# Feed-forward of a hybrid decoder layer: order of the second norm's row, a weight rounding and three stored products

## Chip, cores and metric

The kernel runs on one core of one Trainium2 chip, as one program. Its time is the device time of one execution in microseconds (us); the number compared is the median of several runs.

## What is computed

One layer for 512 prompt tokens and 32 sample tokens (8 sequences of 4), model width 1024: a Conformer convolution branch and an mLSTM branch, merged by gates, then the part that the change is in:

```python
x = x + rmsnorm(jnp.einsum('btd,de->bte', mix, w_o), g_post_mix)
hf = rmsnorm(x, g_pre_ff)
ff = jnp.einsum('btf,fd->btd', jnp.square(jax.nn.relu(jnp.einsum('btd,df->btf', hf, w_ff1) + b_ff1)), w_ff2) + b_ff2
x = x + rmsnorm(ff, g_post_ff)
```

`w_ff1` is 1024 x 4096 and `w_ff2` is 4096 x 1024. `rmsnorm` divides by the root of the mean square over the 1024 features. All is float32.

## The kernel before

Activations lie with features on the 128 partitions and all 544 tokens (`TT`) along a row. Every weight matrix is cut into chunks of 1024 x 128 that arrive in one stream of 176 chunks. For float32 precision each chunk is split in two: `hi` on ScalarE (ACT) rounds it from `wraw` to `whi` (L511), `lo` on VectorE (DVE) subtracts to `wlo` (L846). SyncE's queue (SP) loads chunks into two `wraw` buffers and waits for DVE's roundings; `whi` and `wlo` are rings of four. A product of one chunk with the activations (`part`, `product`, L1311) is three terms (hi x hi, hi x lo, lo x hi) for each of 8 feature tiles, each in two pieces of 256 and 288 columns: 24 groups of two matmuls. Products are written in turn to two PSUM slots. `chunk_done` counts finished products, `drained[s]` counts how often slot `s` has been emptied, and TensorE (PE) waits for `drained[s]` before it writes the slot again. On each engine the instructions run in the order of the program; there is no scheduler.

The feed-forward part takes `w_ff1` in two halves (`f`), each with 16 chunks up and 16 chunks down (`HID` is 16). Up products of the first half begin before the norm of their input is known: the operand is `x * g_pre_ff` without the norm's row `rst`, and each product is multiplied by `rst` afterwards. The first three chunks are multiplied side by side, tile by tile as the operand appears, into the two slots and the spare banks of `side`. ACT copies these three to `kept`. The sums of squares (`column_sums`) follow the fourth product on PE, and `root(4, ...)` on ACT makes `rst` out of them (a table load L524, a logarithm L526, an exponential L528).

Before the change ACT copies and rounds in turn, and then takes the root:

```python
for k in range(3):
    act.wait_ge(chunk_done, C_FF + k + 1)
    act.activation(kept[:, k:k + 1, :], slot(k) if k < 2 else spare(), ACT.Copy).then_inc(drained[k % 2], 1)
    hi(0, 4, C_FF + 4 + k)
root(4, stat_ready, 2)
```

For every up product there is then a chain between DVE and ACT: DVE multiplies by `rst` into `fr` (L1266 for the stored ones, L1269 for the fourth, L1280 in the loop), ACT applies bias and ReLU (L791), the square (L793) and a rounding copy to `hidhi` (L795), and DVE subtracts to `hidlo` (L1260). The three stored products go through it first, then the fourth, and then a loop (`Fori`) of three turns of four products follows, which also rounds the weights of the product three ahead. `hid_hi` and `hid_lo` count finished tiles. The down products (`double`) use all 16 tiles, and their first turn waits tile by tile for `hid_lo`.

Of the kernel before, what the change touches and what calls it, by code (L numbers as in the profile page):

```python
# [32 lines left out]
HID = 16  # L33
# [9 lines left out]
C_FF = C_OUT + KT  # L43
# [18 lines left out]
S_FF = S_OUT + KT // 2  # L62
# [51 lines left out]
def hybrid_layer(nc, xT, wstream, w_gates, cols, b_gates, b_v, w_dw, hist, c_in, n_in, m_in,  # L114
                 yT, conv_p, conv_s, c_p, n_p, m_p, c_s, n_s, m_s):
    f32, f32r = mybir.dt.float32, mybir.dt.float32r
    ALU = mybir.AluOpType
# [5 lines left out]
    with ctx:  # L123
# [180 lines left out]
        def c(name, j):  # L304

            return col[:, bass.ds(COLS[name] + j, 1)]

        def tile(buf, j, lo=0, n=TT):

            return buf[:, bass.ds(j, 1), lo:lo + n]  # L310
# [23 lines left out]
        def own_columns(ap):  # L334

            return bass.AP(ap.tensor, ap.offset, [ap.ap[0], [NS + DEC_T, DEC_B], [1, DEC_T]])

        def spare(lo=0, hi=TT):
            return across(side[:, 2:4, :], lo, hi).rearrange("p (a t) -> p a t", a=1)

# [4 lines left out]
        def slot(s, lo=0, hi=TT):  # L345

            return across(psum[s][:, :, :], lo, hi).rearrange("p (a t) -> p a t", a=1)
# [157 lines left out]
        def _(act):  # L505
            def hi(i, per, k):

                act.wait_ge(raw_in[k % 2], 8 * per * i + 16 * (k // 2 + 1))
                if k >= RING:
                    act.wait_ge(chunk_done, per * i + (k - RING + 1))  # L510
                act.activation(whi[:, k % RING, :, :], wraw[:, k % 2, :, :], ACT.Copy).then_inc(hi_done, 1)  # L511
# [6 lines left out]
                    apart(act)  # L518
                act.activation(fr[:, k:k + 1, :], src, ACT.Square).then_inc(sq_ready, 1)

            def root(n, sums, count):


                act.preload_act_table_set("natural_log_exp_and_others")  # L524
                act.wait_ge(sums, count)
                act.activation(rst[:, :], across(side[:, 0:2, :]), ACT.Ln, bias=eps[:, :], scale=1.0 / D_MODEL).then_inc(ms_ready, 1)  # L526
                act.wait_ge(ms_ready, n)
                act.activation(rst[:, :], rst[:, :], ACT.Exp, scale=-0.5).then_inc(root_ready, 1)  # L528
# [254 lines left out]
            for k in range(3):  # L783
                act.wait_ge(chunk_done, C_FF + k + 1)
                act.activation(kept[:, k:k + 1, :], slot(k) if k < 2 else spare(), ACT.Copy).then_inc(drained[k % 2], 1)
                hi(0, 4, C_FF + 4 + k)
            root(4, stat_ready, 2)

            def hidden(n, i, k):

                act.activation(fr[:, k % 2, :], fr[:, k % 2, :], ACT.Relu, bias=c("b_ff1", n)).then_inc(hid_pos, 1)  # L791
                act.wait_ge(hid_pos, n + 1)
                act.activation(fr[:, 2 + k % 2, :], fr[:, k % 2, :], ACT.Square).then_inc(hidsq_ready, 1)  # L793
                act.wait_ge(hidsq_ready, n + 1)
                act.activation(tile(hidhi, 4 * i + k), fr[:, 2 + k % 2:3 + k % 2, :], ACT.Copy).then_inc(hid_hi, 1)  # L795

            for k in range(4):
                if k < 3:
                    act.wait_ge(hid_scaled, k + 1)
                else:  # L800
                    act.wait_ge(drained[1], S_FF + 2)
                hidden(k, 0, k)

            for f in range(2):
                cf = C_FF + PERHALF * f
                sf = S_FF + S_HALF * f
                with act.Fori(1 - f, HID // 4) as i:
                    for k in range(4):
                        hi(i, 4, cf + k + 3)
                        act.wait_ge(drained[k % 2], 2 * i + (sf + k // 2 + 1))  # L810
                        hidden(4 * i + (HID * f + k), i, k)

                def down(i, ks):
                    for k in range(4):
                        if k in ks:
                            hi(i, 4, cf + HID + k + 3)
                        if k % 2 == 1:
                            j = 2 * i + k // 2
                            if f == 0:
                                act.wait_ge(chunk_done, 4 * i + (cf + HID + k + 1))  # L820
                                act.activation(tile(sgm, j), slot(k // 2), ACT.Identity, bias=c("b_ff2", j)).then_inc(drained[k // 2], 1)
                            else:
                                act.wait_ge(drained[k // 2], i + (sf + HID // 2 + 1))
                                squares(4 * KT + j, tile(y, j), k // 2)

                turns = KT // 2 - f
                with act.Fori(0, turns) as i:
                    down(i, range(4))
                if f == 1:
                    down(turns, range(1))  # L830
# [4 lines left out]
        def _(dve):  # L835
# [411 lines left out]
            for j in range(KT):  # L1247
# [2 lines left out]
                V.tensor_tensor(sqs[:, :], sqs[:, :], fr[:, j % 4, :], ALU.add).then_inc(sq_added, 1)  # L1250
                if j == 3:
                    lo(0, 4, C_FF + 3)
            for k in range(3):
                lo(0, 4, C_FF + 4 + k)
            dve.wait_ge(root_ready, 4)

            def remainder(n, i, k):

                dve.wait_ge(hid_hi, n + 1)
                V.tensor_tensor(tile(hidlo, 4 * i + k), fr[:, 2 + k % 2:3 + k % 2, :], tile(hidhi, 4 * i + k).bitcast(f32),  # L1260
                                ALU.subtract).then_inc(hid_lo, 1)

            for k in range(4):
                if k < 3:
                    dve.wait_ge(drained[k % 2], S_FF + k // 2 + 1)
                    V.tensor_tensor(fr[:, k % 2:k % 2 + 1, :], kept[:, k:k + 1, :], rst3, ALU.mult).then_inc(hid_scaled, 1)  # L1266
                else:
                    dve.wait_ge(chunk_done, C_FF + 4)
                    V.tensor_tensor(fr[:, 1:2, :], slot(1), rst3, ALU.mult).then_inc(drained[1], 1)  # L1269
                remainder(k, 0, k)  # L1270
            n = mark(V.memset(sqs[:, :], 0.0))
            dve.wait_ge(dve_step, n)
            for f in range(2):
                cf = C_FF + PERHALF * f
                sf = S_FF + S_HALF * f
                with dve.Fori(1 - f, HID // 4) as i:
                    for k in range(4):
                        lo(i, 4, cf + k + 3)
                        dve.wait_ge(chunk_done, 4 * i + (cf + k + 1))
                        V.tensor_tensor(fr[:, k % 2:k % 2 + 1, :], slot(k % 2), rst3, ALU.mult).then_inc(drained[k % 2], 1)  # L1280
                        remainder(4 * i + (HID * f + k), i, k)

                def down(i, ks):
                    for k in range(4):
                        if k in ks:
                            lo(i, 4, cf + HID + k + 3)
                        if k % 2 == 1 and f == 1:
                            s, j = k // 2, 2 * i + k // 2
                            dve.wait_ge(chunk_done, 4 * i + (cf + HID + k + 1))
                            V.tensor_tensor(tile(y, j), slot(s), tile(sgm, j), ALU.add).then_inc(drained[s], 1)  # L1290
                            dve.wait_ge(sq_ready, j + (4 * KT + 1))
                            dve.wait_ge(sq_added, j + 4 * KT)
                            V.tensor_tensor(sqs[:, :], sqs[:, :], fr[:, s, :], ALU.add).then_inc(sq_added, 1)

                turns = KT // 2 - f
                with dve.Fori(0, turns) as i:
                    down(i, range(4))
                if f == 1:
                    down(turns, range(1))
# [9 lines left out]
        def _(pe):  # L1309
# [297 lines left out]
            for f in range(2):  # L1607
                cf = C_FF + PERHALF * f
                sf = S_FF + S_HALF * f
                if f == 0:  # L1610
                    ring(0, 4, cf + 2)
                    for s in range(2):
                        free(s, sf)
                    for kt in range(KT):
                        pe.wait_ge(opnd_lo, 3 * KT + kt + 1)
                        for w in range(3):
                            ins = part(w, w, ahi, alo, kt)
                            if kt == KT - 1:
                                ins.then_inc(chunk_done, 1)
                    alternate(0, 3, cf, sf, ahi, alo)  # L1620
                    pe.wait_ge(sq_added, 4 * KT)
                    column_sums(sqs, 0).then_inc(stat_ready, 1)
                with pe.Fori(1 - f, HID // 4) as i:
                    for k in range(4):
                        alternate(i, k, cf, sf, ahi, alo)
                with pe.Fori(0, KT // 2) as i:
                    for k in range(4):
                        double(i, k, cf + HID, sf + HID // 2, hidhi, hidlo, (hid_lo, HID * f))
            pe.wait_ge(sq_added, 5 * KT)
            column_sums(sqs, 0).then_inc(stat_ready, 1)  # L1630
# [75 lines left out]
```

## Time and profile before

| | us |
|---|---|
| median of three runs | 1310.61 |
| lowest, highest | 1309.87, 1311.29 |
| profiled execution, its own time | 1310.51 |
| profiled execution, its span | 1308.7 |
| PE busy in it | 1255.0 |
| DVE busy in it | 721.6 |
| ACT busy in it | 507.5 |

The span is the time from the first to the last instruction in the profile; the execution's own time is 1.8 us longer. Busy times of the engines overlap. A group of matmuls is shown with the ends modelled, so that each overlaps the next; the distance between starts is the pace.

### The profile page before, as it was taken

Reading aid. Unit: us, or ns where it says so; the run is one execution under the profiler, and the core shown is the slowest. Engines: PE = TensorE matmul, PEld = TensorE weight load, DVE = VectorE, ACT = ScalarE, POOL = GpSimd, SP = SyncE. Lnnn points to the kernel's source line nnn. Section 1 sums busy time; section 2 is a strip of 40 time slices with the busy share of each in tenths; the row PEclk is TensorE's granted clock in tenths of the full one; section 3 lists DMA queues with packets and bytes.
Section 4 is the critical chain, followed back from the end, with each engine's and each line's share of the span. In section 5 each row is a group of like instructions: output and inputs, shape, how many; then the busy total and the mean of one; then the engine's idle time right before and its main releaser. Section 6 shows DMA issues by size and latency. Waiting matters only on the chain.

```text
span 1308.7 us, 23730 instructions
## 1 busy us (share of the span) xinstructions
PE 1255.0 (96%) x9099; PEld 1175.6 (90%) x9099; DVE 721.6 (55%) x970; ACT 507.5 (39%) x750; POOL 74.6 (6%) x135
## 2 busy tenths in 40 slices
PE   6999899999999999999999999997799999999994
PEld 6999877888797888879999999997799999999993
DVE  4252588978878888884455443337443212444324
ACT  5333343353354334334554222235554223554211
POOL 3011201100100110110000000000000000000002
PEclk8999899999999999999999999998899999999997
DMA  6235716514441651531222222430232222222211
GB/s 191 81 110 167 108 33 221 191 49 151 174 166 42 218 189 42 186 136 65 81 97 81 97 80 80 149 99 32 80 96 97 81 95 81 81 96 82 95 48 68
DMA packets 39761, 141.17 MB, mean 108 GB/s; under 512 B 5012, under 2 KB 5524, under 8 KB 39592
## 3 DMA queue, kind: packets, MB, share of 16 engines
q1 hardware_dynamic: 27848, 99.37, 23.8%
q0 software_dynamic: 11872, 41.23, 9.5%
q8 instruction: 29, 0.48, 0.2%
q14 instruction: 12, 0.10, 0.0%
HBM read 118.31 MB, written 22.26 MB: 107 GB/s over the span
## 4 chain that ended last, share of the span: by engine, by line
PE 89%; DVE 4%; ACT 3%; DMA 2%; issue 1%; POOLq 0%; POOL 0%; ACTq 0%; DVEq 0%; SPq 0%
PE product L1311 83%; PE side L1311 6%; DMA wraw<-in_wstream 2%; DVE y L1225 0%; ACT whi L511 0%; DVE sqs L1250 0%; DVE yc L1241 0%; DVE hr L1130 0%; DVE y L1239 0%; DVE crg L1107 0%; DVE wlo L846 0%; DMA x<-in_xT 0%; DVE alo L1235 0%; ACT L674 0%; ACT L524 0%
## 5 line engine op out<-in xcount | busy, mean ns | idle before, releaser
L846 DVE TENSOR_TENSOR wlo<-wraw,whi 128x1024 fp32r<-128x1024 f32 x176 | 215.4, 1224 | 239.8 <-ACT whi L511 234.8
L1311 PE MATMUL product<-ahi,whi 128*128 128x256 f32 x1520 | 320.6, 293 | 18.6 <-DVE fr L1269 7.6
L1311 PE MATMUL product<-ahi,wlo 128*128 128x256 f32 x1520 | 316.8, 290 | 0.0
L1311 PE MATMUL product<-alo,whi 128*128 128x256 f32 x1520 | 315.1, 289 | 0.0
L511 ACT ACTIVATE whi<-wraw 128x1024 fp32r<-128x1024 f32 x176 | 184.5, 1052 | 237.7 <-PE product L1311 177.5
L1311 PEld LDWEIGHTS product<-ahi,whi 128*128 128x128 f32 x1520 | 246.2, 191 | 25.7 <-issue 25.0
L1311 PEld LDWEIGHTS product<-alo,whi 128*128 128x128 f32 x1520 | 245.7, 190 | 0.0
L1311 PEld LDWEIGHTS product<-ahi,wlo 128*128 128x128 f32 x1520 | 245.1, 190 | 0.0
L997 DVE SCALAR_TENSOR_TENSOR accp<-u,wdw,accp 128x512 f32<-128x512 f32 x240 | 163.0, 744 | 0.3
L1311 PE MATMUL product<-hidhi,wlo 128*128 128x256 f32 (+1 forms) x512 | 106.0, 288 | 0.0
L1311 PE MATMUL product<-hidlo,whi 128*128 128x256 f32 (+1 forms) x512 | 105.9, 288 | 0.0
L1311 PE MATMUL product<-hidhi,whi 128*128 128x256 f32 (+1 forms) x512 | 105.0, 286 | 0.0
L1311 PEld LDWEIGHTS product<-hidhi,wlo 128*128 128x128 f32 x512 | 82.1, 189 | 0.0
L1311 PEld LDWEIGHTS product<-hidhi,whi 128*128 128x128 f32 x512 | 81.9, 188 | 0.0
L1311 PEld LDWEIGHTS product<-hidlo,whi 128*128 128x128 f32 x512 | 81.2, 188 | 0.0
L1260 DVE TENSOR_TENSOR hidlo<-fr,hidhi 128x544 f32 (+1 forms) x32 | 23.2, 726 | 79.4 <-ACT hidhi L795 79.4
L1311 PE MATMUL product<-whi,ahi 128*128 128x512 f32 (+1 forms) x160 | 57.8, 361 | 3.7 <-DVE wlo L846 3.7
L1311 PE MATMUL product<-wlo,ahi 128*128 128x512 f32 (+1 forms) x160 | 56.8, 355 | 0.0
L1311 PE MATMUL product<-whi,alo 128*128 128x512 f32 (+1 forms) x160 | 56.6, 354 | 0.0
L791 ACT ACTIVATE fr<-fr,col 128x544 f32<-128x544 f32 x32 | 24.0, 750 | 82.7 <-DVE fr L1280 77.6
L1311 PE MATMUL product<-bhi,wlo 128*128 128x256 f32 (+1 forms) x256 | 53.0, 288 | 0.0
L1311 PE MATMUL product<-mhi,wlo 128*128 128x256 f32 (+1 forms) x256 | 53.0, 288 | 0.0
(260 smaller groups left out, 1660.0 us busy)
## 6 DMA issues: line engine op xcount, KB each, us to landing
wraw<-in_wstream SPq DMA_DIRECT2D x176, 512.0 KB, 3.3
crg<-in_c_in POOLq DMA_DIRECT2D x32, 512.0 KB, 5.8
out_c_s<-crg POOLq DMA_DIRECT2D x32, 512.0 KB, 2.9
hb<-head_rows POOLq DMA_DIRECT2D x4, 580.0 KB, 5.5
x<-in_xT SPq DMA_DIRECT2D x4, 544.0 KB, 5.6
sgm<-in_xT SPq DMA_DIRECT2D x1, 2176.0 KB, 9.0
out_yT<-y SPq DMA_DIRECT2D x8, 272.0 KB, 2.1
out_c_p<-cst POOLq DMA_DIRECT2D x4, 512.0 KB, 7.8
```

Of the source, the lines that this page charges most:

```text
L511: act.activation(whi[:, k % RING, :, :], wraw[:, k % 2, :, :], ACT.Copy).then_inc(hi_done, 1)
L791: act.activation(fr[:, k % 2, :], fr[:, k % 2, :], ACT.Relu, bias=c("b_ff1", n)).then_inc(hid_pos, 1)
L846: V.tensor_tensor(wlo[:, k % RING, :, :], wraw[:, k % 2, :, :], whi[:, k % RING, :, :].bitcast(f32), ALU.subtract).then_inc(lo_done, 1)
L997: ins = V.scalar_tensor_tensor(sum_, src, w, sum_, ALU.mult, ALU.add)
L1260: V.tensor_tensor(tile(hidlo, 4 * i + k), fr[:, 2 + k % 2:3 + k % 2, :], tile(hidhi, 4 * i + k).bitcast(f32), ALU.subtract).then_inc(hid_l ...
L1311: return pe.matmul(out, lhsT, rhs, start=start, stop=stop, skip_group_check=check)
```

## The change

In the feed-forward part: ACT copies all three stored products first, then rounds two chunks instead of three, then makes the root without loading its table; DVE then scales the fourth product, which is still in its slot, and that product goes through the chain first. The rounding of the chunk `C_FF + 6` follows it. The three stored products are taken one in each turn of the loop, after that turn's second product. `hidden_at` and `kept_at` give the place of a tile in the new order of the counters. PE waits for 14 subtractions at the head of each turn of the first half's down projection, since the stored tiles 1 and 2 now come late in the count.

```diff
+        def hidden_at(f, i, k):
+            return 4 * i + (HID + k) if f == 1 else 5 * i + (k - 4 + k // 2)
+        def kept_at(i):
+            return 5 * i - 2
...
-            def root(n, sums, count):
-                act.preload_act_table_set("natural_log_exp_and_others")
+            def root(n, sums, count, table=True):
+                if table:
+                    act.preload_act_table_set("natural_log_exp_and_others")
...
             for k in range(3):
                 act.wait_ge(chunk_done, C_FF + k + 1)
                 act.activation(kept[:, k:k + 1, :], slot(k) if k < 2 else spare(), ACT.Copy).then_inc(drained[k % 2], 1)
+            for k in range(2):
                 hi(0, 4, C_FF + 4 + k)
-            root(4, stat_ready, 2)
+            root(4, stat_ready, 2, table=False)
-            for k in range(4):
-                if k < 3:
-                    act.wait_ge(hid_scaled, k + 1)
-                else:
-                    act.wait_ge(drained[1], S_FF + 2)
-                hidden(k, 0, k)
+            act.wait_ge(drained[1], S_FF + 2)
+            hidden(0, 3, 3, 1)
+            hi(0, 4, C_FF + 6)
...
                         hi(i, 4, cf + k + 3)
                         act.wait_ge(drained[k % 2], 2 * i + (sf + k // 2 + 1))
-                        hidden(4 * i + (HID * f + k), i, k)
+                        hidden(hidden_at(f, i, k), 4 * i + k, 4 * i + (HID * f + k), k % 2)
+                        if f == 0 and k == 1:
+                            act.wait_ge(hid_scaled, i)
+                            hidden(kept_at(i), i - 1, i - 1, 0)
...
-            for k in range(3):
+            for k in range(2):
                 lo(0, 4, C_FF + 4 + k)
             dve.wait_ge(root_ready, 4)
-            for k in range(4):
-                if k < 3:
-                    dve.wait_ge(drained[k % 2], S_FF + k // 2 + 1)
-                    V.tensor_tensor(fr[:, k % 2:k % 2 + 1, :], kept[:, k:k + 1, :], rst3, ALU.mult).then_inc(hid_scaled, 1)
-                else:
-                    dve.wait_ge(chunk_done, C_FF + 4)
-                    V.tensor_tensor(fr[:, 1:2, :], slot(1), rst3, ALU.mult).then_inc(drained[1], 1)
-                remainder(k, 0, k)
+            dve.wait_ge(chunk_done, C_FF + 4)
+            V.tensor_tensor(fr[:, 1:2, :], slot(1), rst3, ALU.mult).then_inc(drained[1], 1)
             n = mark(V.memset(sqs[:, :], 0.0))
             dve.wait_ge(dve_step, n)
+            remainder(0, 3, 1)
+            lo(0, 4, C_FF + 6)
...
                         V.tensor_tensor(fr[:, k % 2:k % 2 + 1, :], slot(k % 2), rst3, ALU.mult).then_inc(drained[k % 2], 1)
-                        remainder(4 * i + (HID * f + k), i, k)
+                        if f == 0 and k == 1:
+                            V.tensor_tensor(fr[:, 0:1, :], tile(kept, i - 1), rst3, ALU.mult).then_inc(hid_scaled, 1)
+                        remainder(hidden_at(f, i, k), 4 * i + k, k % 2)
+                        if f == 0 and k == 1:
+                            remainder(kept_at(i), i - 1, 0)
...
                 with pe.Fori(0, KT // 2) as i:
                     for k in range(4):
+                        if f == 0 and k == 0:
+                            pe.wait_ge(hid_lo, HID - 2)
                         double(i, k, cf + HID, sf + HID // 2, hidhi, hidlo, (hid_lo, HID * f))
```

## Rows read from the trace of the kernel before

**Rows 1.** The page's span and its busy time of PE.

```profile
span 1308.7 us, 23730 instructions
PE 1255.0 (96%) x9099; PEld 1175.6 (90%) x9099; DVE 721.6 (55%) x970; ACT 507.5 (39%) x750; POOL 74.6 (6%) x135
```

**Rows 2.** Waits of PE from 880 to 970: us in total, times, longest.

```profile
PE product L1311 <- DVE fr L1269: 7.6, 1, 7.6
PE product L1311 <- DVE alo L1235: 5.9, 1, 5.9
PE product L1311 <- ACT kept L785: 0.8, 1, 0.8
```

**Rows 3.** Timeline of PE: start, us, instruction, idle before.

```profile
911.66 0.41 PE L1311 MATMUL side<-ahi,wlo 128*128 128x256 f32 x2
912.85 0.48 PE L1311 MATMUL product<-ahi,whi 128*128 128x256 f32 x2 [0.77 <-ACT kept L785]
...
918.91 1.08 PE L1311 MATMUL side<-sqs,ones 128*128 128x256 f32 x4
919.61 0.63 PE L1311 MATMUL product<-ahi,whi 128*128 128x256 f32 x2
...
925.57 0.41 PE L1311 MATMUL product<-ahi,wlo 128*128 128x256 f32 x2
933.55 0.80 PE L1311 MATMUL product<-ahi,whi 128*128 128x256 f32 x2 [7.57 <-DVE fr L1269]
...
936.83 0.40 PE L1311 MATMUL product<-alo,whi 128*128 128x256 f32 x2
...
1000.97 0.42 PE L1311 MATMUL product<-hidhi,whi 128*128 128x256 f32 x2
```

**Rows 4.** Windows: length, busy us of each engine, PE's granted clock, DMA.

```profile
933.00:936.00 3.00, 2.45 (x11) 2.48 (x12) 0.81 (x2) 2.50 (x4) 0.00 (x0) 0.50 0.00 0
...
940.00:945.00 5.00, 5.00 (x42) 5.00 (x42) 2.58 (x3) 2.84 (x4) 0.00 (x0) 1.00 0.32 99
```

**Rows 5.** Timeline of ACT.

```profile
910.62 0.62 ACT L785 ACTIVATE kept<-product 128x544 f32<-128x544 f32 x1 [0.60 <-PE product L1311]
...
912.09 0.62 ACT L785 ACTIVATE kept<-product 128x544 f32<-128x544 f32 x1
914.05 1.06 ACT L511 ACTIVATE whi<-wraw 128x1024 fp32r<-128x1024 f32 x1 [1.35 <-DMA wraw<-in_wstream]
...
918.21 1.06 ACT L511 ACTIVATE whi<-wraw 128x1024 fp32r<-128x1024 f32 x1 [2.59 <-DMA wraw<-in_wstream]
919.29 1.28 ACT L524 ACT_TABLE_LOAD   x1
920.58 0.71 ACT L526 ACTIVATE rst<-side,eps 128x544 f32<-128x544 f32 x1
921.33 0.66 ACT L528 ACTIVATE rst<-rst 128x544 f32<-128x544 f32 x1
...
941.27 1.04 ACT L511 ACTIVATE whi<-wraw 128x1024 fp32r<-128x1024 f32 x1
944.34 0.75 ACT L791 ACTIVATE fr<-fr,col 128x544 f32<-128x544 f32 x1 [2.03 <-DVE fr L1280]
...
946.47 1.04 ACT L511 ACTIVATE whi<-wraw 128x1024 fp32r<-128x1024 f32 x1
```

**Rows 6.** Chain that ended last, one transfer in it.

```profile
914.89 3.30 DMA wraw<-in_wstream
```

**Rows 7.** Timeline of DVE.

```profile
922.02 0.73 DVE L1266 TENSOR_TENSOR fr<-kept,rst 128x544 f32<-128x544 f32 x1 [1.49 <-ACT rst L528]
924.94 0.72 DVE L1260 TENSOR_TENSOR hidlo<-fr,hidhi 128x544 fp32r<-128x544 f32 x1 [2.20 <-ACT hidhi L795]
...
932.69 0.71 DVE L1269 TENSOR_TENSOR fr<-product,rst 128x544 f32<-128x544 f32 x1
```

More of the change, by code:

```diff
@@ L785, in _, with hidden @@
                 act.activation(kept[:, k:k + 1, :], slot(k) if k < 2 else spare(), ACT.Copy).then_inc(drained[k % 2], 1)
+            for k in range(2):
                 hi(0, 4, C_FF + 4 + k)
-            root(4, stat_ready, 2)
-            def hidden(n, i, k):
-                act.activation(fr[:, k % 2, :], fr[:, k % 2, :], ACT.Relu, bias=c("b_ff1", n)).then_inc(hid_pos, 1)
+            root(4, stat_ready, 2, table=False)
+            def hidden(n, j, bias, b):
+                act.activation(fr[:, b, :], fr[:, b, :], ACT.Relu, bias=c("b_ff1", bias)).then_inc(hid_pos, 1)
                 act.wait_ge(hid_pos, n + 1)
-                act.activation(fr[:, 2 + k % 2, :], fr[:, k % 2, :], ACT.Square).then_inc(hidsq_ready, 1)
+                act.activation(fr[:, 2 + b, :], fr[:, b, :], ACT.Square).then_inc(hidsq_ready, 1)
                 act.wait_ge(hidsq_ready, n + 1)
-                act.activation(tile(hidhi, 4 * i + k), fr[:, 2 + k % 2:3 + k % 2, :], ACT.Copy).then_inc(hid_hi, 1)
-            for k in range(4):
-                if k < 3:
-                    act.wait_ge(hid_scaled, k + 1)
-                else:
-                    act.wait_ge(drained[1], S_FF + 2)
-                hidden(k, 0, k)
+                act.activation(tile(hidhi, j), fr[:, 2 + b:3 + b, :], ACT.Copy).then_inc(hid_hi, 1)
+            act.wait_ge(drained[1], S_FF + 2)
+            hidden(0, 3, 3, 1)
+            hi(0, 4, C_FF + 6)
             for f in range(2):
@@ L1252, in _, with remainder @@
                     lo(0, 4, C_FF + 3)
-            for k in range(3):
+            for k in range(2):
                 lo(0, 4, C_FF + 4 + k)
             dve.wait_ge(root_ready, 4)
-            def remainder(n, i, k):
+            def remainder(n, j, b):
                 dve.wait_ge(hid_hi, n + 1)
-                V.tensor_tensor(tile(hidlo, 4 * i + k), fr[:, 2 + k % 2:3 + k % 2, :], tile(hidhi, 4 * i + k).bitcast(f32),
+                V.tensor_tensor(tile(hidlo, j), fr[:, 2 + b:3 + b, :], tile(hidhi, j).bitcast(f32),
                                 ALU.subtract).then_inc(hid_lo, 1)
-            for k in range(4):
-                if k < 3:
-                    dve.wait_ge(drained[k % 2], S_FF + k // 2 + 1)
-                    V.tensor_tensor(fr[:, k % 2:k % 2 + 1, :], kept[:, k:k + 1, :], rst3, ALU.mult).then_inc(hid_scaled, 1)
-                else:
-                    dve.wait_ge(chunk_done, C_FF + 4)
-                    V.tensor_tensor(fr[:, 1:2, :], slot(1), rst3, ALU.mult).then_inc(drained[1], 1)
-                remainder(k, 0, k)
+            dve.wait_ge(chunk_done, C_FF + 4)
+            V.tensor_tensor(fr[:, 1:2, :], slot(1), rst3, ALU.mult).then_inc(drained[1], 1)
             n = mark(V.memset(sqs[:, :], 0.0))
             dve.wait_ge(dve_step, n)
+            remainder(0, 3, 1)
+            lo(0, 4, C_FF + 6)
             for f in range(2):
```

## The prediction

> **What bounds the kernel now.** I read the page's totals first. TensorE (PE) is busy 1255.0 of 1308.7 us [rows 1], so only its idle time and its slow stretches can be won back. The profiled execution took 1310.51 us, 1.8 more than its span. The waits of PE around the start of the feed-forward part come next: of the stretch from 880 to 970, three waits are named [rows 2]. The 5.9 us for `alo` lie ahead of everything the diff touches. The other two are in its reach: 7.6 us for the scaling of the fourth chunk (L1269) and 0.8 us for the copy to `kept` (L785).
>
> The timeline of PE places them [rows 3]. I call the products of the first half's up projection 1 to 16; 1 to 3 run side by side. The last group of product 3 starts at 911.66; product 4 starts only at 912.85, the column sums of the second norm at 918.91, product 5 at 919.61. Its last group starts at 925.57, and product 6 starts at 933.55. The windows show the granted clock beside it [rows 4]: 0.50 in 933 to 936, right after the long idle time, and 1.00 in 940 to 945; these are the levels 1.2 and 2.4 GHz. Seven groups lie between 933.55 and 936.83, the other 257 groups of products 6 to 16 between 936.83 and 1000.97 [rows 3].
>
> Why product 6 waits is in the timelines of ScalarE (ACT) and VectorE (DVE). ACT copies product 2 to `kept` at 912.09, behind a weight rounding; it rounds the chunk for product 7 at 918.21, since its DMA took 3.30 us to land [rows 5, 6]; then come a table load, the logarithm and the exponential [rows 5]. DVE scales stored product 1 at 922.02, waits for ACT to make its operand, subtracts at 924.94, and two more stored products follow in the same way. Only at 932.69 does it scale product 4, whose slot product 6 needs [rows 7]. From 941 on ACT and DVE keep a rhythm of 5.20 us a chunk (one rounding to the next, 941.27 to 946.47 [rows 5]), which is shorter than PE's.
>
> **The change, part by part.** *The copies to `kept` ahead of the roundings.* Product 2 ends three groups of 0.25 after product 1; ACT's copy of product 1 began right behind its product at 910.62 [rows 5], so the copy of product 2 can begin at 911.36 and ends 0.62 later, at 911.98. Between the end of that copy and product 4 lie 912.85 - 912.71 = 0.14 us now [rows 3, 5], so product 4 starts at 912.12: 0.73 us earlier. Both ends: nothing, or 0.94 if it starts one group behind 911.66. I take 0.73, which is the row's own 0.14.
>
> *The row of the norm.* Product 4 to the sums and to product 5 takes 6.76 us as now [rows 3], so the sums start at 918.18 and product 5 at 918.88. The sums end 1.08 us later, 919.26. ACT is free by then: its second rounding of this stretch still starts at 914.05, when its DMA lands, and ends at 915.1 [rows 5]; the third is now behind the root. With 0.71 and 0.66 us for the two activations [rows 5] and 0.02 us ahead of each, `rst` is there at 920.67 instead of 921.99. The removed table load (1.28 us, one instruction) isn't on PE's path here.
>
> On that load the row shows 1.28 us [rows 5], with the logarithm 0.01 us behind it and the load 0.02 us behind the rounding. The Trainium skill, "ScalarE: Activation LUTs", section "What ACT_TABLE_LOAD costs", gives 1283 ns plus a drain of about 1380 ns; the trace agrees with the first figure and shows no such drain. The same page ("Table sets") says that a compiler pass puts a load ahead of every activation that needs one. If it put this one back, `rst` would be there at 921.95 by the row and 923.3 by the page; the sum would be the same by both, for the margin below is larger.
>
> *Product 4 scaled first.* DVE starts at 920.69, needs 0.74 as for the stored product [rows 7], and with PE's 0.14 product 6 could start at 921.6. Product 5 starts at 918.88 and holds PE 6.21 us (925.57 + 0.25 - 919.61 [rows 3]), so product 6 starts at 925.09 and waits for nothing; margin 3.5 us. It starts 8.46 us earlier than now, 0.73 of it from the first part and 7.73 from the stall.
>
> *The clock.* With no idle time ahead of product 6 the slow stretch goes: seven groups took 3.28 us and take 7 x 0.25 = 1.75 at the full clock, 1.53 us. That full pace is (1000.97 - 936.83)/257 = 0.2496 a group, 5.99 us a product [rows 3].
>
> *The three stored products, one per turn.* They take from each turn of four products one DVE scaling, three ACT instructions and one DVE subtraction more. The ACT part is 2.15 us: 944.34 to 946.47 from the start of a chunk's three ACT instructions to the next rounding [rows 5], and 0.02 for handing over. Beside the plain chunk's work only ACT's part adds to the rhythm, since DVE scales the stored product while ACT is at the other operand: 4 x 5.20 + 2.15 = 22.95 us a turn, against PE's 4 x 5.99 = 23.96. All in a row with DVE's 0.74 and 0.72 [rows 7] it would be 24.4, 0.5 too many a turn.
>
> What is queued behind the stored product matters in the first turn. After `rst`, ACT makes product 4's operand (921.4 to 923.6), rounds for product 7 (to 924.7; DVE's part to 925.9, needed at 931.08: margin 5.2) and for product 8; DVE scales product 5 at 927.1 to 927.8, needed by product 7 at 931.08: margin 3.2. Product 6 is scaled by 933.1, needed at 937.07: 3.9. Then the first stored product is in the way, and product 7 is scaled at about 933.1 + 5.20 + 2.15 = 940.5, needed by product 9 at 943.05: margin 2.5, the smallest. Even the 24.4 us of the serial order eat only 1.5 of it in three turns. So this part costs nothing; if the cover were gone it would cost its 2.15 us three times, 6.4. SP's queue only waits for DVE's roundings; the chunk for product 9 can be requested at 925.9 and lands 3.3 later [rows 6], 929.2, while ACT asks for it at about 930: no wait, by 0.8; if that were lost, the 2.5 would have to go as well before PE waits.
>
> *The wait for 14 subtractions* at the head of the four turns of the down projection. Products 6 to 16 end at 925.09 + 11 x 5.99 = 990.98. The third stored product's subtraction lies behind product 14, done at 979.0, by 0.7 + 2.15 + 2.15 + 0.75: 984.8, margin 6.2. The wait itself has no row. Every product of [rows 3] has such waits inside its 0.2496 a group, which speaks for 0; the upper end is 4 x 0.14 = 0.6. I take 0. Register work for the new counters: the same, 0, with 0.14 a step as the upper end, still inside the margins.
>
> **Sum.** 0.73 + 7.73 + 1.53 = 9.99 us, nothing to subtract. The profiled execution would take 1310.51 - 9.99 = 1300.52 us; the median of the runs is 0.10 above the profiled one, so 1300.6.
>
> **Rivals.** *The turn becomes too long.* For it: the margin of 2.5 is small, and four chunks and a stored product fill 23 of 24 us. Against: even the serial order fits. It decides from 24.8 us a turn on (2.5 over three turns). At 26 us a turn PE would wait 3 x 2.04 - 2.5 = 3.6 us: 1304.2; with waits long enough for a slow stretch of 1.5 as in [rows 4], 1305.7.
>
> *The wait only moves.* Product 7's weights are now rounded behind the root and one operand. Were they late by the 5.2 of margin and 7 to 9 us more, the time would be 1300.6 + 7 to 9 + 1.5 for the clock, 1309.1 to 1311.1. What speaks against it is that each step ahead of them has a row.
>
> *Slower.* The new wait for 14 subtractions holds all of the down projection, although its first eight steps need only tiles 0 to 7. From 6.2 us of delay of the third stored product on each us costs one; it decides from 6.2 + 10.0 - 1.5 + 2.6 = 17.3 us late. At 20 us late PE stands 13.8 us more and loses 1.5 to the clock: 1300.6 + 15.3 = 1315.9. The delay would have to come from a turn of over 30 us, for which no row speaks.
>
> **How the numbers follow.** About 0.2% (2.6 us) is what a measurement of this kernel tells from no change. The forecast case gets 0.87, a turn too long 0.07, a moved wait 0.04, slower 0.02. The first two are faster by more than 2.6 us, the third is the same: 0.94, 0.04, 0.02. The case's own spread: the first term from 0.94 to 0 (-0.2, +0.7), 0.6 for the waits, and the runs before lay 0.7 on either side of their median. I take 1299.4 to 1302.4; it reaches the mild end of the first rival and leaves out no more than 2 in 10.
>
> **What would show it.** Right: product 4 at about 912.1; no table load between it and the logarithm; `rst` at about 920.7; product 6 straight behind product 5 at about 925.1 at clock 1.00; no idle time of PE from there to the last column sums; the first `hidhi` matmul at 991.0 instead of 1000.97. Wrong: PE waiting for the scaling of a slot within the loop, ACT's roundings spaced so that a turn passes 24.8 us, or a wait for `hid_lo` ahead of the down projection.

## The result, and the profile after

The first four runs of the changed kernel took 1299.62, 1293.23, 1299.56 and 1295.79 us: median 1297.67, against 1310.24 for four runs of the kernel before; ratio 0.9913, 95% interval 0.9884 to 0.9942. (The ratios in this text are estimated together with their intervals and are not the quotients of the medians beside them; here that quotient is 0.9904.) Forecast were 1300.6, between 1299.4 and 1302.4, so the median lies 1.7 us below the range. Over all runs made for this text the changed kernel has 23 (seven of them profiled), median 1301.03, from 1293.23 to 1304.53; the kernel before has 97, median 1311.47, from 1307.13 to 1316.19. The difference of these medians is 10.44 us; the forecast difference was 9.99.

The profiled execution of the changed kernel took 1299.62 us, its span 1297.8. First PE's timeline, the answer to [rows 3]:

```profile
910.93 0.41 PE L1320 MATMUL side<-ahi,wlo 128*128 128x256 f32 x2
911.41 0.49 PE L1320 MATMUL product<-ahi,whi 128*128 128x256 f32 x2
...
917.47 1.08 PE L1320 MATMUL side<-sqs,ones 128*128 128x256 f32 x4
918.17 0.63 PE L1320 MATMUL product<-ahi,whi 128*128 128x256 f32 x2
...
924.38 0.41 PE L1320 MATMUL product<-ahi,whi 128*128 128x256 f32 x2
...
990.28 0.41 PE L1320 MATMUL product<-hidhi,whi 128*128 128x256 f32 x2
```

Product 6 starts at 924.38, 6.21 us behind product 5, where before it started 13.94 us behind. This execution is 0.73 us early already at the end of the products side by side (910.93 against 911.66), in code that both kernels share; take that off the forecast times and they read 911.39, 924.36 and 990.25, beside 911.41, 924.38 and 990.28 measured.

The waits of PE from 880 to the end (us in total, times, longest), and the window around the start of product 6 (the last numbers are clock, DMA share, GB/s):

```profile
PE product L1320 <- DVE alo L1244: 5.9, 1, 5.9
PE side L1320 <- DVE sqs L1302: 2.3, 1, 2.3
```

```profile
924.00:930.00 6.00, 6.00 (x51) 6.00 (x50) 3.46 (x4) 3.60 (x5) 0.00 (x0) 1.00 0.53 171
```

Of the three waits of [rows 2] only the one for `alo` is left. The second line is the wait ahead of the last column sums, which the kernel before has as well. PE is full at clock 1.00 where [rows 4] show 0.50. ACT and DVE around the root and in the first turn, beside [rows 5] and [rows 7]:

```profile
909.89 1.38 ACT L794 ACTIVATE kept<-product 128x544 f32<-128x544 f32 x2 [1.48 <-PE product L1320]
911.38 0.63 ACT L794 ACTIVATE kept<-side 128x544 f32<-128x544 f32 x1
911.90 2.00 ACT L519 ACTIVATE whi<-wraw 128x1024 fp32r<-128x1024 f32 x2
918.59 0.71 ACT L535 ACTIVATE rst<-side,eps 128x544 f32<-128x544 f32 x1 [4.69 <-PE side L1320]
919.34 0.66 ACT L537 ACTIVATE rst<-rst 128x544 f32<-128x544 f32 x1
920.79 0.75 ACT L801 ACTIVATE fr<-fr,col 128x544 f32<-128x544 f32 x1 [0.79 <-DVE fr L1273]
```

```profile
920.03 0.72 DVE L1273 TENSOR_TENSOR fr<-product,rst 128x544 f32<-128x544 f32 x1 [4.67 <-ACT rst L537]
...
926.18 0.72 DVE L1285 TENSOR_TENSOR fr<-product,rst 128x544 f32<-128x544 f32 x1
...
931.41 0.72 DVE L1285 TENSOR_TENSOR fr<-product,rst 128x544 f32<-128x544 f32 x1
932.05 0.72 DVE L1287 TENSOR_TENSOR fr<-kept,rst 128x544 f32<-128x544 f32 x1
...
938.77 0.72 DVE L1285 TENSOR_TENSOR fr<-product,rst 128x544 f32<-128x544 f32 x1
...
943.99 0.72 DVE L1285 TENSOR_TENSOR fr<-product,rst 128x544 f32<-128x544 f32 x1
...
949.39 0.72 DVE L1285 TENSOR_TENSOR fr<-product,rst 128x544 f32<-128x544 f32 x1
...
972.51 0.72 DVE L1285 TENSOR_TENSOR fr<-product,rst 128x544 f32<-128x544 f32 x1
...
983.88 0.73 DVE L1269 TENSOR_TENSOR hidlo<-fr,hidhi 128x544 f32 x1 [1.37 <-ACT hidhi L805]
```

The three copies stand ahead of the roundings, and ACT now waits 4.69 us for the sums, where before PE waited for the scaling of product 4. The prediction had the second rounding at 914.05, behind its transfer; here both run from 911.90 to 913.90, which changes nothing in the sum. From one scaling in the loop to the next are 5.23, 7.36 and 5.22 us: the middle one holds the stored product, 2.13 us more, as forecast (2.15). A whole turn takes 23.21 us (926.18 to 949.39) and then 23.12 us (949.39 to 972.51); forecast were 22.95, and 24.8 was the sign of being wrong. The last line shown is the fourteenth subtraction, that of the third stored product. It ends at 984.61, 5.7 us ahead of the first down product; forecast was a margin of 6.2.

### The profile page after: what moved, and what is told of

It is laid out like the page before. It is cut to its first block, busy times and chain, and to the rows that moved or that the text cites. A ratio compares the mean times of both kernels' runs of the same rounds, so it can differ in the third digit from the quotient of the medians.

```text
span 1297.8 us, 23746 instructions
## 1 busy us (share of the span) xinstructions
PE 1253.1 (97%) x9099; PEld 1173.7 (90%) x9099; DVE 720.9 (56%) x970; ACT 505.9 (39%) x749; POOL 74.8 (6%) x135
## 4 chain that ended last, share of the span: by engine, by line
PE 92%; DVE 2%; ACT 2%; DMA 2%; issue 1%; POOLq 0%; POOL 0%; ACTq 0%; DVEq 0%; SPq 0%
PE product L1320 85%; PE side L1320 7%; DMA wraw<-in_wstream 1%; DVE y L1234 0%; DVE hr L1139 0%; DVE crg L1116 0%; ACT whi L519 0%; DMA x<-in_xT 0%; ACT L683 0%; DVE wlo L855 0%; PE side L1469 0%; ACT fr L527 0%; ACT L533 0%; ACT sqh L713 0%; ACT rst L535 0%
## 5 line engine op out<-in xcount | busy, mean ns | idle before, releaser
L1320 PE MATMUL product<-mhi,whi 128*128 128x256 f32 (+1 forms) x256 | 52.9, 288 | 0.0
```

Of the source, the lines that this page charges most:

```text
L1320: return pe.matmul(out, lhsT, rhs, start=start, stop=stop, skip_group_check=check)
```

## The experiments

Each median stands beside runs of the kernel before on the same chip; a ratio has its 95% interval. "The stretch" is the distance on PE from the start of the second norm's column sums to the first down product. It contains everything that the diff does behind product 4 up to the down products, and nothing before it: 82.06 us in the profile of before (1000.97 - 918.91), 72.81 in that of the changed kernel.

### The two kernels again

Theory A: the runs differ by slow clock stretches in shared code. Theory B: they differ inside the rewritten loop.

> The changed kernel once more. In its profiled execution the change itself is worth 9.96 us, as forecast, yet single runs lay up to 6.4 us below it, and the mean granted clock of a run follows its time (0.986 at 1299.6, 0.990 at 1293.2). Theory A (slow clock elsewhere): the runs differ in how many of the slow stretches near 20, 156, 642 and 890 us they have; a lower time comes with a higher mean clock, by about 1.3 us for each 0.001, and the windows show which stretch is missing. Theory B (the loop): the runs differ within the stretch that the change rewrote; then the distance from product 4 to the first down product is not 78.9 us in a run of another total.

> The kernel before once more, for its spread and clocks. Theory A, in its plain form (the slow stretches are in code that both kernels share): the runs spread as those of the changed kernel do, some at 1304 to 1307 us with a clock above 0.985. Theory B: they stay within 1309 to 1311.5.

The changed kernel: 1300.75 us (1298.91 to 1302.56, 6 runs), ratio 0.9912 (0.9897 to 0.9928), the stretch 72.81. The kernel before: 1311.54 (1309.94 to 1314.54, 12 runs), beside it 29 further runs at 1311.55 (1308.52 to 1316.19). Theory B is out for the changed kernel, whose low single runs did not come back. For the kernel before neither form came true: no run lay at 1304 to 1307 us, and its runs spread upwards, past 1311.5. The stretch of before was 83.54 this time, 1.48 longer than in the execution that the prediction rests on. The rows show where. PE's timeline, and the window at 936 us in which the first execution had clock 0.87:

```profile
917.70 1.08 PE L1311 MATMUL side<-sqs,ones 128*128 128x256 f32 x4
...
932.59 0.79 PE L1311 MATMUL product<-ahi,whi 128*128 128x256 f32 x2 [7.82 <-DVE fr L1269]
...
1001.24 0.41 PE L1311 MATMUL product<-hidhi,whi 128*128 128x256 f32 x2
```

```profile
936.00:939.00 3.00, 3.00 (x17) 3.00 (x16) 1.86 (x2) 0.81 (x2) 0.00 (x0) 0.58 0.15 29
```

From product 6 to the first down product it is 68.65 us here and 67.42 in [rows 3].

### Only the copies moved

```diff
             for k in range(3):
                 act.wait_ge(chunk_done, C_FF + k + 1)
                 act.activation(kept[:, k:k + 1, :], slot(k) if k < 2 else spare(), ACT.Copy).then_inc(drained[k % 2], 1)
+            for k in range(3):
                 hi(0, 4, C_FF + 4 + k)
```

> Before, with the three copies to kept ahead of the three roundings, and nothing else. Product 4 starts 0.7 us earlier, but the third rounding still stands between it and the root, and its transfer is requested 0.25 us later; product 6 starts 0.2 us later than before. Time 1310.4 to 1310.8, no gain. Were product 4's start worth its 0.7 by itself, 1309.8.

1311.27 us (1308.85 to 1314.14, 12 runs), ratio 0.9997 (0.9987 to 1.0008): no change, as expected. ACT's timeline and PE's wait:

```profile
918.69 1.06 ACT L511 ACTIVATE whi<-wraw 128x1024 fp32r<-128x1024 f32 x1 [3.81 <-DMA wraw<-in_wstream]
919.77 1.28 ACT L524 ACT_TABLE_LOAD   x1
```

```profile
PE product L1312 <- DVE fr L1270: 8.5, 1, 8.5
```

The wait for the copy is gone, and the wait for product 4's scaling is longer by as much as was gained. The third rounding still waits for its transfer in front of the root. By this run the 0.7 us can count only once the next wait is gone.

### Only the fourth product first

```diff
+            act.wait_ge(drained[1], S_FF + 2)
+            hidden(0, 0, 3, 3)
+            for k in range(3):
+                act.wait_ge(hid_scaled, k + 1)
+                hidden(k + 1, 0, k, k)
...
+            dve.wait_ge(chunk_done, C_FF + 4)
+            V.tensor_tensor(fr[:, 1:2, :], slot(1), rst3, ALU.mult).then_inc(drained[1], 1)
+            remainder(0, 0, 3)
+            for k in range(3):
+                V.tensor_tensor(fr[:, k % 2:k % 2 + 1, :], kept[:, k:k + 1, :], rst3, ALU.mult).then_inc(hid_scaled, 1)
+                remainder(k + 1, 0, k)
...
                     for k in range(4):
+                        if f == 0 and k == 0:
+                            pe.wait_ge(hid_lo, 4)
```

Left out are the old loops that these lines replace and a parameter that picks each chunk's bias. As in the changed kernel PE also gets a wait ahead of the down products, here for 4 subtractions.

> Before, with the fourth product scaled first, but the three stored products straight behind it, ahead of the loop; the root and its table load stay. By the steps of the prediction the wait only moves: product 6 starts at once (about 925.8), product 7 waits for the scaling of product 5, which now lies behind four chains of 3.55 us, until about 938.9, and a slow stretch of 1.5 us follows. Time 0.7 us below before (1309.5). If scaling the fourth product first were by itself what brings the gain, about 1301.

1311.88 us (1308.83 to 1312.95, 12 runs), ratio 0.9996 (0.9985 to 1.0007). The 0.7 us expected lies inside this interval, so the time alone decides nothing. The wait moved, as expected; DVE's timeline and PE's wait:

```profile
923.86 0.72 DVE L1263 TENSOR_TENSOR fr<-product,rst 128x544 f32<-128x544 f32 x1 [2.00 <-ACT rst L528]
...
940.12 0.72 DVE L1277 TENSOR_TENSOR fr<-product,rst 128x544 f32<-128x544 f32 x1
```

```profile
PE product L1308 <- DVE fr L1277: 6.5, 1, 6.5
```

Product 4 is scaled at once, but product 5 only 16.3 us later, behind four chains, and PE waits 6.5 us for it ahead of product 7. The stretch is 80.92 us, 1.1 less than in the profile of before. So scaling the fourth product first is not enough; with the stored products straight behind it, it is worth nothing that the runs can tell.

### The root's two parts undone, one at a time

The table load put back (`root(4, stat_ready, 2)`), and then the third rounding as well ahead of the root.

> The changed kernel with the table load of the fourth root put back. If the load is off PE's path, rst is 1.28 us later (margin 3.5 us for product 6, 2.7 in the loop) and PE never waits for it: the time is that of the changed kernel, about 1300.5 us. If the load were a term of the gain, 1301.8. Theory A on the scatter (slow stretches elsewhere decide single runs) also says that lone runs below 1297 us, as the changed kernel had twice, can appear here too.

1301.31 us (1300.08 to 1302.39, 5 runs), ratio 0.9921 (0.9908 to 0.9934), the stretch 72.81. Not even `rst` is later: ACT's timeline has the load 2.9 us ahead of the logarithm, inside the wait for the sums. From the start of the sums to the logarithm it is 1.12 us (918.42 - 917.30), as in the changed kernel (918.59 - 917.47).

```profile
914.27 1.28 ACT L533 ACT_TABLE_LOAD   x1
918.42 0.71 ACT L535 ACTIVATE rst<-side,eps 128x544 f32<-128x544 f32 x1 [2.86 <-PE side L1320]
```

> The changed kernel with the first part undone: the third rounding stands ahead of the root again, with the table load. The steps of the prediction give rst at about 922.1 us on the clock of before, product 6 free at 923.0, needed at 925.1; every later margin shrinks by under 1 us from 2.5. Time as the changed kernel, 1300.5. The rival, that the row of the norm must be early for the gain: 1302 to 1304.

1301.98 us (1300.48 to 1304.16, 6 runs), ratio 0.9925 (0.9912 to 0.9937), the stretch 72.80 us. ACT's timeline, with the column sums at 920.26:

```profile
920.59 1.06 ACT L519 ACTIVATE whi<-wraw 128x1024 fp32r<-128x1024 f32 x1 [3.90 <-DMA wraw<-in_wstream]
921.67 1.28 ACT L533 ACT_TABLE_LOAD   x1
922.96 0.71 ACT L535 ACTIVATE rst<-side,eps 128x544 f32<-128x544 f32 x1
923.71 0.66 ACT L537 ACTIVATE rst<-rst 128x544 f32<-128x544 f32 x1
```

The row comes 4.11 us behind the start of the sums instead of 2.53, and PE doesn't see it. Taking the norm's row ahead of the rounding only widens margins here.

### The three stored products at one place

The loops of the first half are written out, and all three stored products follow the second product of the first turn.

```diff
+                        if f == 0 and k == 1 and i == 1:
+                            for t in range(1, 4):
+                                act.wait_ge(hid_scaled, t)
+                                hidden(kept_at(t), t - 1, t - 1, (t - 1) % 2)
...
```

> The changed kernel with all three stored products behind the second product of the first turn instead of one per turn (both loops of the first half written out). Two more chains of 2.15 us on ACT stand ahead of the scaling of product 7. In the trace of the changed kernel that scaling ends 2.8 us before product 9 could start, so PE waits about 1.5 us there, and nowhere else: 1302.0 if the clock stays up, 1303.5 if it falls. If the one-per-turn spread is not needed and only the place behind product 4 matters: 1300.5.

1302.43 us (1301.43 to 1303.92, 5 runs), ratio 0.9927 (0.9914 to 0.9939), the stretch 73.60: 0.79 longer. PE does wait at the place named, for 0.5 us instead of 1.5. PE's and DVE's timelines:

```profile
946.44 0.52 PE L1337 MATMUL product<-ahi,whi 128*128 128x256 f32 x2 [0.52 <-DVE fr L1292]
```

```profile
934.59 0.72 DVE L1292 TENSOR_TENSOR fr<-product,rst 128x544 f32<-128x544 f32 x1
...
945.66 0.72 DVE L1292 TENSOR_TENSOR fr<-product,rst 128x544 f32<-128x544 f32 x1
...
950.67 0.72 DVE L1292 TENSOR_TENSOR fr<-product,rst 128x544 f32<-128x544 f32 x1
```

Product 7 is scaled 24.79 us behind the start of the sums (945.66 - 920.87) where the changed kernel has 21.30 (938.77 - 917.47). These 3.49 us use up the margin of 2.9 and put PE over the edge, so the margin at this place is real and small. It also shows how little the spreading itself is worth: one place for all three costs 0.8 us of the stretch, and the medians do not tell the two apart. The excess was overrated because the written-out code has a rhythm of 5.01 us a product (950.67 - 945.66) where the loop has 5.22, and takes 11.07 over the place with three stored products: 2.02 for each.

### The clock's term alone

The kernel before, with 28 groups of matmuls behind product 5, which go into spare banks and are read by nobody.

```diff
+                if f == 0:
+                    alternate(1, 0, cf, sf, ahi, alo)
+                    free(0, sf + 2)
+                    ring(1, 4, cf + 1)
+                    fill(28, ahi, 1)
+                    for k in range(1, 4):
+                        alternate(1, k, cf, sf, ahi, alo)
-                with pe.Fori(1 - f, HID // 4) as i:
+                with pe.Fori(2 * (1 - f), HID // 4) as i:
```

> Before, with 28 groups of matmuls into the spare banks behind product 5, whose result nobody reads; they fill 7.0 of the 7.6 us for which PE waits there. It measures the clock's term of the sum by itself. The prediction took 1.53 us from one execution; the second profiled execution of before has 3.0 by the distance from the column sums to the first down product (83.5 against 82.1 us). Theory C (the term was mis-sized): product 6 starts when it did, at full clock, and the time falls by 1.5 to 3.0, median 1309.0 beside 1311.6. Rival: the slow stretch costs nothing of its own or comes in spite of the filling: 1311.5.

1309.19 us (1307.50 to 1311.73, 11 runs) beside 1311.47, ratio 0.9983 (0.9975 to 0.9992). PE's timeline and its window across the start of product 6:

```profile
920.23 1.08 PE L1311 MATMUL side<-sqs,ones 128*128 128x256 f32 x4
...
935.10 0.48 PE L1311 MATMUL product<-ahi,whi 128*128 128x256 f32 x2 [0.85 <-DVE fr L1269]
...
1001.07 0.41 PE L1311 MATMUL product<-hidhi,whi 128*128 128x256 f32 x2
```

```profile
930.00:936.00 6.00, 5.15 (x42) 4.96 (x41) 2.72 (x4) 3.05 (x5) 0.00 (x0) 1.00 0.00 0
```

The same wait with the clock kept up: product 6 starts 14.87 us behind the sums, in the three profiles of before 14.64, 14.89 and 14.80. From there to the first down product it is 65.97 us, where those have 67.42, 68.65 and 67.26. So the clock costs 1.45, 2.68 and 1.29 us, 1.8 in the mean, and by the medians of the runs 2.3, for which the interval allows 1.0 to 3.3.

### Once more, and four more profiled executions

> The changed kernel a third time. The stretch from the column sums to the first down product is 72.8 us again, and the median 1300 to 1301.5. The question is whether runs at 1293 to 1296 us, of which there were two among the first four, come again; they would show a mean clock of 0.988 or more.

> The kernel before a third time. Median 1311 to 1312; the stretch from the column sums to the first down product between 82.0 and 83.6 us, which is where the size of the clock's term varies. If theory C is right its excess over 72.8 + 7.7 us of waiting is between 1.5 and 3.0.

1302.13 us (1297.92 to 1304.53, 6 runs), ratio 0.9918 (0.9902 to 0.9935), and 1311.45 (1307.13 to 1313.08, 11 runs). The stretches: 72.80 and 82.06. Beyond 72.8 + 7.7 us the three profiles of before have 1.56, 3.04 and 1.56 us; 1.5 to 3.0 was expected. The changed kernel's median is 0.6 above the 1301.5 expected. No run lay at 1293 to 1296. The two lowest, 1297.92 and 1298.51, have the mean clock of 0.988.

> The changed kernel, one of four more profiled executions. Shown so far: the stretch that the change rewrote takes 72.8 us in all three profiles, so the scatter (1293.2 to 1304.5 us) lies elsewhere. Theory A1: it is made of the wait for a transfer near 156 us (3.3 to 6.0 us in the profiles) and of the slow stretch near 642 us (0 to 2 us); then a run's time follows from these two within 1 us, and a run below 1297 needs both at their low ends or an earlier gain. Theory A2: a third place contributes as much, and the distances between the marks at 20, 156, 642, 884 and 918 us will show which.

For the other three the expectation was shorter, and the same each time:

> As the look before it: the rewritten stretch at 72.8 us; the total explained by the marks at 20, 156, 642, 884 and 918 us.

> As the look before it: the rewritten stretch at 72.8 us; the total explained by the marks at 20, 156, 642, 884 and 918 us.

> As the look before it: the rewritten stretch at 72.8 us; the total explained by the marks at 20, 156, 642, 884 and 918 us.

1300.88, 1302.20, 1301.58 and 1301.68 us; the first also timed: median 1301.48, 4 runs, ratio 0.9919 (0.9902 to 0.9935). The marks of all seven profiles of the changed kernel: the starts of the first product, of the product behind the transfer near 156 us, of the three sums, of the first down product and of the last sums.

```
profile       first   wait  156     642     884     918     down    last sums
first         20.81   3.32  156.14  641.85  882.44  917.47  990.28  1280.13
again         20.32   5.26  157.46  642.68  884.89  919.89  992.70  1282.55
third         19.96   5.63  158.09  643.48  885.68  920.89  993.69  1283.55
fourth        20.75   3.83  156.52  642.07  884.21  918.34  991.15  1281.00
fifth         19.59   5.85  156.56  642.67  884.81  918.88  991.69  1281.54
sixth         20.19   5.59  157.08  642.48  884.55  919.42  992.23  1282.08
seventh       20.15   5.97  157.41  642.01  884.19  919.45  992.26  1282.12
```

From 918 to down every one has 72.80 or 72.81 us, and from there to the last sums 289.85 or 289.86. All scatter is ahead of 918, in code that both kernels share. Its parts: the mark at 156 moves by 2.0 us, 156 to 642 takes 484.6 to 486.1, 642 to 884 takes 240.6 in the first profile and 242.1 to 242.2 in the six others, 884 to 918 takes 34.1 to 35.3. Theory A1's two places, 156 and 642, carry most of it but not all, so A2 holds too. At 156 it is a transfer, which took 9.3 to 10.4 us in the seven profiles; PE's wait in the first profile of the changed kernel and in that of the fourth product first, and the transfer behind each in the chain that ended last:

```profile
156.14 0.58 PE L1320 MATMUL product<-whi,ahi 128*128 128x256 f32 x1 [3.32 <-DVE wlo L855]
```

```profile
144.40 9.27 DMA wraw<-in_wstream
```

```profile
158.08 0.58 PE L1308 MATMUL product<-whi,ahi 128*128 128x256 f32 x1 [6.03 <-DVE wlo L845]
```

```profile
145.60 10.01 DMA wraw<-in_wstream
```

The low ends of all parts together give 156.14 + 484.60 + 240.59 + 34.07 + 72.81 + 289.85 + 17.67 for the tail + 1.8 outside the span = 1297.5 us. The runs at 1295.79 and 1293.23 lie below even that. Their mean granted clocks, 0.988 and 0.990, point to fewer slow stretches: the five lowest of the 23 runs, up to 1298.91 us, have 0.987 to 0.990, and all others 0.983 to 0.986. But no profile covers the two, and which stretch they saved stays open.

### A version that beats both

Theory A also names places to gain. The column sums at 642 us, for which PE waits 2.24 us, were put into the middle of the next product (of eight tiles, behind the fourth):

```diff
-            pe.wait_ge(sq_added, 2 * KT)
-            column_sums(sqs, 0).then_inc(stat_ready, 1)
-            with pe.Fori(0, KT // 4) as i:
+            w = ring(0, 4, C_GATE + KT)
+            free(0, S_GATE + KT // 2)
+            for kt in range(KT):
+                if kt == 4:
+                    pe.wait_ge(sq_added, 2 * KT)
+                    column_sums(sqs, 0).then_inc(stat_ready, 1)
+                ins = part(0, w, ahi, alo, kt)
+            ins.then_inc(chunk_done, 1)
+            for k in range(1, 4):
+                alternate(0, k, C_GATE + KT, S_GATE + KT // 2, ahi, alo)
+            with pe.Fori(1, KT // 4) as i:
```

> The changed kernel with one more edit, at 642 us: the column sums ahead of the second gate products, for which PE waits 2.24 us, are put into the middle of the first of those products. Theory A says that this removes 2.24 us of waiting and with it the slow stretch that most runs have there, some 1.5 to 2 us more: 1296.5 to 1297, and profiles with no slow stretch near 642. If that stretch comes whatever PE does: 1298.3. If the later norm row stalls PE (slack 0.1 us by the trace), about 1300.

1297.86 us (1296.86 to 1299.30, 4 runs) beside 1311.59, ratio 0.9897 (0.9881 to 0.9912); the changed kernel's was 0.9912 to 0.9919. The windows, first of this kernel, then of the changed kernel's third profile, with PE's timeline of that profile:

```profile
639.00:645.00 6.00, 6.00 (x46) 5.84 (x46) 0.73 (x1) 3.69 (x5) 0.00 (x0) 1.00 0.20 78
```

```profile
642.00:648.00 6.00, 4.52 (x20) 4.11 (x21) 1.51 (x2) 4.51 (x6) 0.00 (x0) 0.72 0.01 3
```

```profile
643.48 1.87 PE L1320 MATMUL side<-sqs,ones 128*128 128x256 f32 x4 [2.24 <-DVE sqs L863]
```

No wait and no slow stretch; the distance from 156 to 884 is 723.36 us instead of 726.3 to 728.3. The median lies between the 1296.5 to 1297 expected and the rival's 1298.3, and would not decide by itself; the window does.

To this, 22 groups of unread matmuls were added in the 5.9 us wait ahead of the feed-forward part (`fill(22, bhi)`):

> The changed kernel with the column sums inside the gate product and 22 groups of unread matmuls (5.5 us) in the 5.9 us that PE waits ahead of the feed-forward part. Products 1 to 3 then start at full clock. Now the eight tiles take 20.8 us instead of 8 x 2.25 = 18.0, but DVE delivers a tile only every 2.09 us. By theory A 2.4 us less than with the sums inside alone: 1295.4, and the scatter of single runs narrows to about 2 us. If DVE's pace held the tiles anyway: 1297.9.

1296.12 us (1293.89 to 1297.11, 4 runs) beside 1311.47, ratio 0.9879 (0.9864 to 0.9893), the fastest here. The windows of this kernel and of the one without the filling:

```profile
885.00:891.00 6.00, 5.60 (x45) 5.41 (x44) 5.86 (x10) 3.90 (x6) 0.00 (x0) 1.00 0.00 0
```

```profile
885.00:891.00 6.00, 2.66 (x12) 2.69 (x13) 5.86 (x10) 3.89 (x6) 0.00 (x0) 0.50 0.00 0
```

The clock is up, but from the start of the first product to the column sums it is 25.07 us against 25.77 (913.24 - 888.17, 914.11 - 888.34): 0.7 us of the 2.4 expected. Here the slow stretch was short without the filling too: the clock in 888 to 900 is 0.86 there, and 0.57 to 0.72 in the profiles of the changed kernel. From the mark at 884 to that at 918 the filled kernel has 33.20 us, and those profiles 34.1 to 35.3. DVE is busy 5.86 of 6 us in both windows shown, which suggests that its pace, not PE's clock, sets most of this part. The medians differ by 1.7 us, but the intervals of the ratios overlap, and four runs spread over 3.2 us where about 2 was expected. So that the filling gains anything is seen in the profiles only.

## Why the mechanism held and the range did not

**The copies first**, forecast 0.73: product 4 follows the last group of product 3 by 0.48 us instead of 1.19, 0.71. The copies alone gave nothing, so it can be a term only in the sum; no run takes them back out of the changed kernel.

**The stall of product 6**, forecast 7.73: it is gone, and product 6 follows product 5 by 6.21 us. Together with the clock the stretch shrank by 82.06 - 72.81 = 9.25; forecast was 7.73 + 1.53 = 9.26.

**The stored products, one per turn**, forecast at nothing: shown. PE has no wait in the loop in any of the seven profiles, and 2.13 us for a stored product. Product 7 is scaled by 939.49; product 9 could start at 924.38 + 3 x 5.99 = 942.35: margin 2.9, forecast 2.5. Two chains of 2.0 more used it up. The rival that the wait only moves is what happens when the stored products stand straight behind the fourth. The slower rival stayed away: the first down product follows product 6 by 65.90 us, eleven products at 5.99, and from there to the last sums it is 289.85 us as before (1290.82 - 1000.97 there). So the wait for 14 subtractions, put at 0, costs nothing.

**The table load and the early row**, forecast at nothing: shown by undoing each. The statement in passing that a load put back would make `rst` 1.28 us later was wrong, since ACT waits for the sums at that time. It changed no number. In the late root's rows the logarithm starts at 922.96, 0.01 us behind the load's end, as in [rows 5]. The longer cost in the Trainium skill ("ScalarE: Activation LUTs", "What ACT_TABLE_LOAD costs") is not seen in these rows.

**The clock**, forecast 1.53, is the term of the sum that was sized too low, if by little. It was read off one execution, [rows 3, 4], and varies: 1.45, 2.68 and 1.29 us in three, 1.8 in the mean and 2.3 by medians, whose interval holds 1.53 as well. With the 0.71 and the stretches of before (82.06, 83.54, 82.06 against 72.81) the gain is 10.0, 11.4 and 10.0 us by the three profiles.

**The step that failed** is the last one before the range, "the runs before lay 0.7 on either side of their median". The scatter of three runs was taken for the scatter of the result. Over 97 runs that kernel lies between 1307.1 and 1316.2 around 1311.47, 0.9 above the 1310.61 that the sum used, and the changed one between 1293.2 and 1304.5. In the seven profiles of the changed kernel all of the scatter lies ahead of 918, in code that both kernels share. A range of 3 us for a median of few runs had no room for that: the four groups of runs of the changed kernel have medians of 1297.67, 1300.75, 1302.13 and 1301.48. With all runs the median is 1301.03, inside the range and 0.4 from the forecast, helped by two errors that cancel in part: the base too low by 0.9, the gain too small by 0.45. That the forecast is this close is in part luck. The four first runs held the two lowest of 23; why, stays open, as said above. Some of it may belong to that group of runs, since the kernel before was low in it too, 1310.24 against 1311.45 to 1311.98 in all later groups.

## What to carry to other kernels

When several engines pass one buffer on, scale first what sits in the scarce buffer (here a PSUM slot), and put what is already stored into turns where the helpers have time left; count the turn, and the smallest margin, before doing so. A wait of the engine that sets the pace is worth its length plus what the clock takes behind it, and that second part has to be read from more than one execution. Take the scatter for a range from the sources that the trace shows (a slow stretch present or absent, a transfer near other traffic), not from the spread of three runs.

## What was not expected of the hardware

After a wait of PE as short as 2.24 us, ahead of the sums at 642 us, the granted clock fell in six of seven profiles of the changed kernel and in all three of the kernel before; it stayed at 1.00 in one. This is worth 1.5 us (642 to 884: 242.1 to 242.2 against 240.6). The window of the one profile, to be set beside the 0.72 shown above:

```profile
642.00:648.00 6.00, 6.00 (x46) 5.84 (x47) 1.90 (x2) 5.19 (x6) 0.00 (x0) 1.00 0.01 3
```

The cost of the stall's slow stretch differed by a factor of two between executions of one kernel. The same chain of instructions on ACT and DVE took 5.22 us a product inside a loop and 5.01 written out.
